# The two parts of x moved by 128 bytes in SBUF, in a two-block transformer kernel on one core

## What is computed

```python
u, gt = jnp.split(x @ ffn_w_in, 2, axis=-1)
...
return (jax.nn.silu(a) * u) @ ffn_w_out
...
return (jax.nn.silu(x @ wg) * (x @ wu)) @ wd
```

## Time and profile before

| | before |
|---|---|
| median of 3 runs | 2161.82 us (2157.68 to 2164.14) |
| profiled execution, own time | 2162.65 us |
| its span | 2160.9 us |
| busy: matmuls, weight loads | 2096.1 us (97%), 2041.5 us (94%) |
| busy: VectorE, ScalarE, GpSimd | 1427.8, 1013.5, 60.4 us |
| mean granted TensorE clock | 0.991 |
| matmuls | 17332 |

### The profile page before, as it was taken

One profiled execution on the slowest core, in us unless ns is written; L12 is line 12 of the kernel. 1 busy time (PEld: TensorE's weight loads), 2 busy tenths in 40 slices (PEclk: granted clock), 3 DMA queues, 4 the chain that ended last, 5 costly groups with the idle time before them and its releaser, 6 DMA issues.

```text
span 2160.9 us, 39287 instructions
## 1 busy us (share of the span) xinstructions
PE 2096.1 (97%) x17332; PEld 2041.5 (94%) x17332; DVE 1427.8 (66%) x1693; ACT 1013.5 (47%) x1198; POOL 60.4 (3%) x58
## 2 busy tenths in 40 slices
PE   7999999999999999998998899999999999999997
PEld 6999999999998999998998899988999999989997
DVE  6655564676776555646777676797655766797664
ACT  5544454444455544544543543445433444454442
POOL 1000000100010000001000000000000000000000
PEclk9999999999999999999999899999999999999999
DMA  5444544455544445434554355533555555534552
GB/s 208 152 161 157 192 179 148 146 195 177 195 160 152 161 157 190 181 132 158 192 194 174 126 192 195 193 118 139 187 184 193 179 195 195 176 118 156 193 192 84
DMA packets 52858, 365.93 MB, mean 169 GB/s; under 512 B 5905, under 2 KB 5905, under 8 KB 9297
## 3 DMA queue, kind: packets, MB, share of 16 engines
q1 hardware_dynamic: 52272, 361.21, 47.0%
q0 software_dynamic: 416, 2.22, 0.3%
HBM read 362.35 MB, written 1.05 MB: 168 GB/s over the span
## 4 chain that ended last, share of the span: by engine, by line
PE 83%; issue 9%; DVE 4%; ACT 3%; POOL 1%; DMA 1%; POOLq 0%; ACTq 0%; SPq 0%
PE accM L1137 48%; PE scoreP L1137 18%; PE outP L1137 8%; PE turnP L1137 8%; DVE wlo L1582 1%; PE turnP L1324 1%; ACT x L829 1%; ACT whi L764 1%; DMA raw<-in_W 1%; ACT ew L949 1%; PE outP L1350 0%; DVE mrs L2137 0%; ACT xh L833 0%; DVE cen L1693 0%; POOL xl L711 0%
## 5 line engine op out<-in xcount | busy, mean ns | idle before, releaser
L1582 DVE TENSOR_TENSOR wlo<-raw,whi 128x2048 fp32r<-128x2048 f32 x336 | 769.2, 2292 | 370.7 <-ACT whi L764 369.6
L764 ACT ACTIVATE whi<-raw 128x2048 fp32r<-128x2048 f32 x336 | 639.8, 1910 | 242.2 <-PE accM L1137 130.5
L1137 PE MATMUL accM<-xh,whi 128*128 128x256 f32 x1152 | 336.9, 292 | 8.1 <-DVE xl L1713 6.0
L1137 PE MATMUL scoreP<-xh,whi 128*128 128x256 f32 x1152 | 323.7, 281 | 11.1 <-DVE xl L1605 5.0
L1137 PE MATMUL accM<-xl,whi 128*128 128x256 f32 x1152 | 322.4, 280 | 0.0
L1137 PE MATMUL accM<-xh,wlo 128*128 128x256 f32 x1152 | 322.4, 280 | 0.0
L1137 PE MATMUL scoreP<-xl,whi 128*128 128x256 f32 x1152 | 321.7, 279 | 0.0
L1137 PE MATMUL scoreP<-xh,wlo 128*128 128x256 f32 x1152 | 321.5, 279 | 0.0
L1137 PE MATMUL accM<-fh,wlo 128*128 128x256 f32 x1056 | 293.2, 278 | 0.0
L1137 PE MATMUL accM<-fh,whi 128*128 128x256 f32 x1056 | 293.2, 278 | 0.0
L1137 PE MATMUL accM<-fl,whi 128*128 128x256 f32 x1056 | 293.2, 278 | 0.0
(11 more groups left out here) (277 smaller groups left out, 4164.8 us busy)
## 6 DMA issues: line engine op xcount, KB each, us to landing
raw<-in_W SPq DMA_DIRECT2D x336, 1024.0 KB, 4.8
biasr<-in_bias SPq DMA_DIRECT2D x16, 256.0 KB, 2.8
raw<-in_memT SPq DMA_DIRECT2D x2, 1024.0 KB, 5.6
cc<-in_consts POOLq DMA_DIRECT2D x1, 1408.0 KB, 7.0
x<-in_xT SPq DMA_DIRECT2D x4, 256.0 KB, 4.4
out<-x SPq DMA_DIRECT2D x4, 256.0 KB, 2.5
c<-in_consts SPq DMA_DIRECT2D x1, 464.5 KB, 6.4
par<-in_par POOLq DMA_DIRECT2D x2, 203.5 KB, 3.6
```

The source lines that it names most:

```text
L764: nc.scalar.activation(whi[:, hi_slot(c), :], raw[:, raw_slot(c), :], ACT.Copy).then_inc(split_hi.sem, 1)
L1137: return nc.tensor.matmul(dst, a, b, start=start, stop=stop, skip_group_check=True)
L1582: v.tensor_tensor(wlo[:, raw_slot(c), :], raw[:, raw_slot(c), :], whi[:, hi_slot(c), :].bitcast(F32), ALU.subtract).then_inc(split_lo.sem, 1)
```

## The change

The two paddings are exchanged in size. Their sum stays, so nothing behind `_trail` moves, and `xh` and `xl` move by 128 bytes.

```diff
         x = sb("x", [P, KT, S])
-        _lead = sb("lead", [P, 48])
+        _lead = sb("lead", [P, 80])
         xh = sb("xh", [P, KT, S], F32R)
         xl = sb("xl", [P, KT, S], F32R)
-        _trail = sb("trail", [P, 80])
+        _trail = sb("trail", [P, 48])
```

## The result

The changed kernel takes 2186.87 us (median of 4 runs, 2183.47 to 2188.91), beside 2162.2 us for the kernel before in the same series. The ratio is 1.0112, 95% interval 1.0077 to 1.0148: slower by 1.1%. The forecast was 2159 us; 2186.87 us lies inside the range given (2148 to 2190), between the first and the second rival, and on the other side of no change.

The account below looks back on a forecast made before the run. The prediction took TensorE to bound the kernel, by the number of matmuls times their pitch. Its terms summed to -3.0 us on the profiled 2162.65 us, 2159.7, hence 2159 us against the median; range 2148 to 2190 us.

Parts of the forecast that it names:

- the first and the second rival: "Each part keeps to its distance" (2179 us, chance 0.18) and "slow from end to end" (2193 us, chance 0.13), both slower.
- The frame: Whole kernel: time is the number of matmuls times their pitch, 113.3 ns fast or 117.8 ns slow.
- fast at 192 stays fast when the stream goes over to 320: Unbroken changes of distance inside the blocks: a fast stream keeps its pitch; each matmul turned would cost 4.45 ns.
- Slow to fast by the second matmul: Going from x at 320 to the hidden layer: a slow stream with its second matmul at 280 ns falls to fast.
- every last block would start with the second one: Blocks from 1210, 1499, 1688 and 1976 us: slow for 168 matmuls, the second of each product at 280 ns, then fast.
- x in kind F outside the blocks: 1088 matmuls fast before, 42 of 45 restarts at 320 slow: +4.5 us, bounds 0 and +4.8.
- kind T on x: Matmuls moved from 320 to 192, 530 slow before: half become fast, -1.2 us, bounds 0 and -2.4.
- the six blocks: Feed-forward blocks: one from 1499 us turns fast, -6.3; three start slow, +2.2; two of the first stack, +0.7 us.
- The gates and branches: Slow stretches with x and y mixed, two holding 1308 matmuls: one of two should fall to fast, -2.9 us.
- Each part keeps to its distance: In the blocks x goes slow at every change and the hidden layer fast again: +17.4 us, 2179 us, chance 0.18.
- slow from end to end: A block that starts slow on x ends slow: +28.2 us and +3.3 outside, 2193 us, chance 0.13.
- The distance does nothing: Restarts at 320 are slow for other reasons: 2162 us, a block or so more or less fast, chance 0.13.

Follow-up runs that it names:

- experiment 2: Kernel before with only the hidden layer moved to distance 320, x kept at 192: 2181.37 us, ratio 1.0086.
- experiment 4: Kernel before with only xl moved to distance 320, xh and the hidden layer kept at 192: 2187.49 us, ratio 1.0131.
- 7: Kernel before with wlo moved 128 bytes from whi; x and hidden layer 192 behind whi, 320 behind wlo: 2141.1 us, ratio 0.993.
- experiment 9: Kernel before with wlo spaced otherwise, x and hidden layer 192 from whi: first 64 from wlo, 2140.33 us; then 448, 2150.28 us.
- experiment 10: Kernel before with 32 float32 between wlo and whi and 32 between xh and xl: 2206.33 us, ratio 1.0245.

## Why the prediction was wrong

- **The frame held.** The time is the number of matmuls times their pitch. Summed over the profiled executions, what the main matmuls take above 113.33 ns each (starts up to 121 ns apart) grew from 33.7 to 56.2 us, by 22.4 of the 24.4 us of span; the rest lies in longer gaps and was not assigned. VectorE's writes of `xl` kept their median of 478 ns.
- **The step that failed** was that fast at 192 stays fast when the stream goes over to 320. The text itself named it as the hinge; its evidence was five of five places from the memory as kind F to kind T. In kind F, in the changed kernel, it turned slow at all 30 places at which a fast hidden layer gave over to x, and at all 20 of the other order in experiment 2. The five of five into kind T, where the weights move and the activations are stationary, said nothing of this. The only place of kind F that would have told did not exist in the trace of before, and I ought to have weighed the restarts themselves (42 of 45 slow at 320) above it. Even they would not have been a proof: 17 of 117 restarts of kind F on x at 320 did become fast in the changed kernel, and all of them stayed fast to the end of their stretch. What fails is the going over into 320, not fast matmuls at 320 as such.
- **Slow to fast by the second matmul** held, though two places were all that the forecast had drawn it from, so luck had a part in it. On its way from x to the hidden layer the stream fell to fast at 30 places, with the second one at 280 ns, and stayed slow at 28, with the first or the third. That every last block would start with the second one held in three of four; the block from 1990 us had the third one there and was slow to its end, as were both blocks of the first stack.
- **The terms.** Forecast and measured, from the excess over the fast pitch: x in kind F outside the blocks, the gates among it, +4.5 - 2.9 and +3.4 us; kind T on x, -1.2 and -1.3 us; the six blocks, -6.3 + 2.2 + 0.7 = -3.4 and +20.5 us (x +18.0, hidden layer +2.5). The gates and branches stayed slow and gave nothing of their -2.9 us. Of the 25.4 us between the forecast sum (-3.0) and these 22.4 us, 23.9 are in the blocks.
- **The rivals.** "Each part keeps to its distance" was the case for three blocks, "slow from end to end" for the other three, and the windows show them as the prediction said they would, some 1290 and 1276. By their own prices that is 3 x 4.7 + 3 x 7.05 = 35.3 us in place of 2 x 7.05 = 14.1, +21.2 us beside the +20.5 measured. They were given 0.18 and 0.13, and a mixture of the two was not considered.
- **The distance is no bystander.** The runs differ in nothing but addresses and take 2140 to 2222 us, so the rival "The distance does nothing", which had 0.13, is wrong for this kernel. Where x and the hidden layer lie at one distance, the pitch goes from 113.3 ns (fast, at 192 and 448) to 120.0 ns (at 0 and 256); by what it does so was not seen. DMA traffic is not needed for the slow pitch: the kernel before has stretches without any at both pitches, here x at 192 (113.4 ns between starts) and z at 320 (117.8 ns), in columns like those of the earlier trace rows:

```profile
26.10:28.70 2.60, 2.60 (x26) 1.00 0.00 0
...
1476.80:1479.40 2.60, 2.60 (x24) 1.00 0.00 0
```

**What stays open.** What the distance acts on is not shown. If only the moving operand and the weights of the next load counted, experiments 4 and 7 would be alike (the pairs are xh with `whi` at 192, xl with `wlo` at 320 in both); one is slow and the other fast. Pairs of one and the same matmul do not order the results either, since the first run of experiment 9 has a third of them at 64, where all together are slow, and is fast. What sets experiment 10 at 120.6 ns is open as well. Nor is it known why a fast stream turns slow on going over to 320 in kind F and not into kind T, though single fast starts at 320 last, and what at a restart picks one of two pitches.

## What to carry to other kernels

Where weights are loaded for each matmul and the profile shows TensorE busy throughout at a full clock, count matmuls per window: different counts in like stretches (1276 and 1326 in 150 us here) mean that the pitch has levels, and padding between buffers is a cheap thing to try (it moved this kernel between 2140.33 and 2221.85 us), for each operand pair by itself, the two parts of the weights among them. A single run or a single trace doesn't judge such a change, since restarts draw between the levels (53 of 120 fast in the kernel before, whose single runs took 2147.66 to 2176.55 us in the four series); a layout where nearly every restart becomes fast shows in the median and in the narrow spread. And five of five places of another kind are no evidence for a place of this kind.

## What the runs showed that I had not expected

- With x and the hidden layer 192 bytes from `whi`, 128 or 384 bytes between `wlo` and `whi` make 2141.1 and 2140.33 us of some 2155 (ratio 0.993 both), where all six blocks of the profiled execution are at 113.3 ns. Over 16 runs these two stay within 2137.86 to 2142.86 us, the kernel before in the same series within 2147.66 to 2169.02.
- The pitch has more than two values: 113.3, 117.3, 117.8, 118.3, 118.6, 118.9, 120.0 and 120.6 ns were seen, each held over whole chunks. Of the distances tried for x and the hidden layer together, 0, 128 and 256 bytes were the slowest, up to +2.8%.
- One operand of three at another distance can set the pitch of all three (experiment 4), or free them all (7 and 9).
